# Two written-out decoder layers with a first norm that is loaded, summed and applied tile by tile

## What is computed

```python
c_act = jax.nn.silu(c)
for l in range(DEPTH):                                   # DEPTH = 2
    mod = (c_act @ ada_w[l] + ada_b[l]).reshape(bsz, 3, 3, D_MODEL)
    h = _rmsnorm(x, ffn1_norm[l]) * (1 + mod[:, 0, 1]) + mod[:, 0, 0]
    x = x + 0.5 * (1 + mod[:, 0, 2]) * ((silu(h @ w1[l]) * (h @ w3[l])) @ w2[l])
    h = mod2(RMSNorm(x));  x = x + (1 + g2) * mixer(h)   # RG-LRU and two attentions
    h = mod3(RMSNorm(x));  x = x + 0.5 * (1 + g3) * swiglu(h)
return _rmsnorm(x, final_norm) * (1 + fm[:, 1]) + fm[:, 0]
```

## Time and profile before

| | us |
|---|---|
| median of 3 runs (lowest to highest) | 2819.32 (2815.86 to 2821.81) |
| the profiled execution, by its own time | 2812.3 |
| its span in the profile | 2810.6 |
| PE, DVE, ACT, POOL busy | 2696.0, 1258.1, 1059.6, 1171.8 |

### The profile page before, as it was taken

The page is one execution under the profiler, slowest core; times in us unless marked ns, Lnnn a source line. Parts: engine busy times, 40 slices in busy tenths (PEclk is TensorE's granted clock), DMA queues, the critical chain, the costliest instruction groups (busy, mean ns, idle before and its releaser), DMA issues.

```text
span 2810.6 us, 35297 instructions
## 1 busy us (share of the span) xinstructions
PE 2696.0 (96%) x13124; PEld 2253.0 (80%) x13124; DVE 1258.1 (45%) x1608; ACT 1059.6 (38%) x1593; POOL 1171.8 (42%) x471
## 2 busy tenths in 40 slices
PE   3999999999999999999989999999999999999998
PEld 3888888878878878888888888888888788888886
DVE  6565337865442234411145553477545421453111
ACT  5222236644443244222242222466443432523223
POOL 2555544532223444454435554354222244355443
PEclk9999999999999999999999999999999999999999
DMA  6555532221112323533335555222122123253333
GB/s 219 210 187 203 173 116 95 88 71 60 61 54 75 98 91 127 173 92 103 97 131 191 198 189 167 89 88 91 60 60 61 46 90 98 77 187 127 103 93 97
DMA packets 91302, 325.73 MB, mean 116 GB/s; under 512 B 10096, under 2 KB 12528, under 8 KB 90864
## 3 DMA queue, kind: packets, MB, share of 16 engines
q1 hardware_dynamic: 91120, 323.35, 35.4%
HBM read 321.21 MB, written 2.10 MB: 115 GB/s over the span
## 4 chain that ended last, share of the span: by engine, by line
issue 54%; POOL 33%; PE 12%; POOLq 0%; ACT 0%; DVE 0%; ACTq 0%; DVEq 0%
POOL w_lo L406 32%; PE bank L1189 4%; PE bank L1187 4%; PE bank L1188 4%; POOL wab_lo L412 1%; POOLq L404 0%; ACT fin L765 0%; POOL tmp L389 0%; DVE fin L1180 0%; DVE x L828 0%; ACTq L113 0%; PE bank L1244 0%; ACT rstd L450 0%; ACT tmp L442 0%; ACT rstd L447 0%
## 5 line engine op out<-in xcount | busy, mean ns | idle before, releaser
L406 POOL TENSOR_TENSOR w_lo<-raw,w_hi 128x1024 fp32r<-128x1024 f32 x443 | 1152.4, 2611 | 1541.5 <-ACT w_hi L436 1540.9
L1187 PE MATMUL bank<-h_hi,w_hi 128*128 128x512 f32 x2240 | 876.3, 391 | 0.5
L1188 PE MATMUL bank<-h_lo,w_hi 128*128 128x512 f32 x2240 | 873.4, 390 | 0.0
L1189 PE MATMUL bank<-h_hi,w_lo 128*128 128x512 f32 x2240 | 873.1, 390 | 0.0
L436 ACT ACTIVATE w_hi<-raw 128x1024 fp32r<-128x1024 f32 x443 | 467.2, 1057 | 987.7 <-PE bank L1189 904.8
L1187 PEld LDWEIGHTS bank<-h_hi,w_hi 128*128 128x128 f32 x2240 | 421.6, 188 | 89.1 <-POOL w_lo L406 1.3
L1189 PEld LDWEIGHTS bank<-h_hi,w_lo 128*128 128x128 f32 x2240 | 421.1, 188 | 88.7
L1188 PEld LDWEIGHTS bank<-h_lo,w_hi 128*128 128x128 f32 x2240 | 421.5, 188 | 87.2
L776 DVE CUSTOM_DVE_ANT_0 ada<-ada,c_act 128x1024 f32<-128x1024 f32 x144 | 254.0, 1771 | 266.5 <-DMA ada<-ada_w 266.5
L1189 PE MATMUL bank<-g_hi,w_lo 128*128 128x512 f32 (+1 forms) x792 | 295.2, 373 | 0.0
L1188 PE MATMUL bank<-g_lo,w_hi 128*128 128x512 f32 (+1 forms) x792 | 292.4, 369 | 0.0
(11 more groups left out here) (208 smaller groups left out, 3057.3 us busy)
## 6 DMA issues: line engine op xcount, KB each, us to landing
raw<-w_units SPq DMA_DIRECT2D x443, 512.0 KB, 3.6
ada<-ada_w SPq DMA_DIRECT2D x144, 512.0 KB, 4.5
ada<-ada_w SPq DMA_DIRECT2D x8, 1024.0 KB, 16.5
x<-x_in SPq DMA_DIRECT2D x4, 512.0 KB, 7.3
wab_raw<-wab SPq DMA_DIRECT2D x2, 1024.0 KB, 5.7
y<-fin SPq DMA_DIRECT2D x8, 256.0 KB, 2.2
c_act<-c_rows SPq DMA_DIRECT2D x1, 512.0 KB, 3.7
vec<-vecs SPq DMA_DIRECT2D x3, 92.5 KB, 3.3
```

The costliest lines, as they stand in the source:

```text
L406: nc.gpsimd.tensor_tensor(w_lo[s][:, :, :], raw[u % RAW][:, :, :], w_hi[s][:, :, :].bitcast(F32), ALU.subtract).then_inc(unit_lo.sem, 1)
L1187: nc.tensor.matmul(o, wh, xh, start=start, stop=False, skip_group_check=True)
L1188: nc.tensor.matmul(o, wh, xl, start=False, stop=False, skip_group_check=True)
L1189: return nc.tensor.matmul(o, wl, xh, start=False, stop=stop, skip_group_check=True)
```

## The change

1. **The layers are written out.** `Fori` becomes a Python loop, so the code of both layers stands one behind the other and waits use constants. The loads, roundings and subtractions of units past the last (three of each at the end) are gone.
2. **Loads.** The rows of `ada_w` are reordered on the host so that piece `k` holds shift and scale of tile `k`. Piece 0 is issued ahead of `x`; each of the four loads of `x` has a semaphore of its own; units 0 to 3 follow, two of them into new buffers `raw0`, each with a piece behind it; pieces 5 to 7 come last.
3. **`c_act` in PSUM.** ACT copies it into banks 4 and 5, joined as `bank45`; the 16 first reductions read it there.
4. **Sum of squares and norm.** ACT squares each tile as it lands; DVE adds without reductions between; one matmul, one Ln and one Exp of 512 tokens replace the first half's.
5. **Tile by tile.** For each `k` DVE makes two reductions, adds the bias to two columns and forms one scale, then subtracts for `h_lo` of the tile before. The product with `rstd` is now POOL's, between the `w_lo` of units 0 to 3. ACT writes the unrounded `h` to PSUM banks 6 and 7. All of it handles 512 tokens at once.
6. **PE.** Each tile is multiplied with units 0 and 1 as it comes, and with units 2 and 3 three tiles later.

```diff
+        raw0 = [at(f"raw0_{i}", 65536 + 4096 * i, [P, UB, P]) for i in range(2)]
...
-        bank = [ctx.enter_context(nc.psum_tensor(f"bank{i}", [P, T], F32)) for i in range(8)]
+        bank = [ctx.enter_context(nc.psum_tensor(f"bank{i}", [P, T], F32))[:, :] for i in range(4)]
+        bank45 = ctx.enter_context(nc.psum_tensor("bank45", [P, 2 * T], F32))
+        bank += [bank45[:, 0:T], bank45[:, T:2 * T]]
+        bank += [ctx.enter_context(nc.psum_tensor(f"bank{i}", [P, T], F32))[:, :] for i in (6, 7)]
...
-            for n in range(0, KD, 2):
-                sp.dma_start(x[:, n:n + 2, :], x_in[n:n + 2].rearrange("n p t -> p n t")).then_inc(x_loaded.sem, 16)
-            for g in range(16 // G0):
+            def first_ada(g):
                 sp.dma_start(ada0[g][:, :, :], ada_w[G0 * g:G0 * g + G0].rearrange("n p t -> p n t"))\
                     .then_inc(ada0_loaded[g].sem, 16)
-                if 2 <= g < 2 + RAW:
-                    sp.dma_start(raw[g - 2][:, :, :], w_units[g - 2]).then_inc(raw_loaded[g - 2].sem, 16)
-            with sp.Fori(0, DEPTH) as l:
-                for u in range(RAW, UNITS + RAW):
+
+            first_ada(0)
+            for n in range(0, KD, 2):
+                sp.dma_start(x[:, n:n + 2, :], x_in[n:n + 2].rearrange("n p t -> p n t"))\
+                    .then_inc(x_loaded[n // 2].sem, 16)
+            for u in range(RAW):
+                sp.dma_start(raw[u][:, :, :], w_units[u]).then_inc(raw_loaded[u].sem, 16)
+                first_ada(u + 1)
+            for u in range(RAW, RING):
+                sp.dma_start(raw0[u - RAW][:, :, :], w_units[u]).then_inc(raw0_loaded[u - RAW].sem, 16)
+                first_ada(u + 1)
+            for g in range(RING + 1, KD):
+                first_ada(g)
+            for l in range(DEPTH):
+                for u in range(RING if l == 0 else RAW, UNITS + RAW):
...
-            for u in range(RAW, AHEAD):
-                load_unit(DEPTH, u, u)
...
-            with gp.Fori(0, DEPTH) as l:
-                for u in range(UNITS):
+            def first_lo(u):
+                gp.wait_ge(unit_hi.sem, u + 1)
+                src = raw[u] if u < RAW else raw0[u - RAW]
+                nc.gpsimd.tensor_tensor(w_lo[u][:, :, :], src[:, :, :], w_hi[u][:, :, :].bitcast(F32),
+                                        ALU.subtract).then_inc(unit_lo.sem, 1)
+
+            def first_xr(k):
+                if k >= 2:
+                    gp.wait_ge(hf_0.sem, k - 1)
+                nc.gpsimd.tensor_tensor(tmp[k % 2][:, :], x[:, k, :], rstd[:, :], ALU.mult).then_inc(xr_0.sem, 1)
+
+            first_lo(0)
+            gp.wait_ge(rstd_0.sem, 1)
+            first_xr(0)
+            first_lo(1)
+            first_xr(1)
+            first_xr(2)
+            first_lo(2)
+            first_xr(3)
+            first_lo(3)
+            for k in range(4, KD):
+                first_xr(k)
+            for l in range(DEPTH):
+                for u in range(RING if l == 0 else 0, UNITS):
                     lo(l, u)
                     for c in range(KD):
                         if u == U_X(c) + 3:
                             wab_lo_part(l, c)
-            for u in range(AHEAD):
-                lo(DEPTH, u)
...
+            def first_h(k):
+                act.wait_ge(nscale_0.sem, k + 1)
+                act.wait_ge(xr_0.sem, k + 1)
+                shift, scale = mod[:, k:k + 1], nscale[:, 0, k:k + 1]
+                A(h_hi[:, k, :], tmp[k % 2][:, :], ACT.Identity, bias=shift, scale=scale).then_inc(hh_0.sem, 1)
+                if k >= 2:
+                    act.wait_ge(hl_0.sem, k - 1)
+                A(bank[6 + k % 2][:, :], tmp[k % 2][:, :], ACT.Identity, bias=shift, scale=scale).then_inc(hf_0.sem, 1)
...
+            act.wait_ge(silu_c.sem, 1)
+            A(bank45[:, :], c_act[:, :], ACT.Copy).then_inc(c_wide.sem, 1)
...
-            act.wait_ge(x_loaded.sem, 16 * KD // 2)
-            for n in range(KD - 1):
-                square(0, -1, n)
-            square(0, -1, KD - 1, HALF[0])
-            square(0, -1, KD - 1, HALF[1])
-            norm(0, -1, 0)
-            for u in range(-AHEAD, 0):
-                tick(0, u)
-            with act.Fori(0, DEPTH) as l:
-                h_round(l, -1, 0, 0, ((2, 0),))
-                norm(l, -1, 1)
-                h_round(l, -1, 0, 1)
+            for n in range(KD):
+                if n % 2 == 0:
+                    act.wait_ge(x_loaded[n // 2].sem, 16)
+                if n >= 3:
+                    act.wait_ge(sqsum_0.sem, n - 2)
+                A((tmp[n % 2] if n else sqsum)[:, :], x[:, n, :], ACT.Square).then_inc(sq_0.sem, 1)
+            first_tick(0)
+            act.wait_ge(sumsq_0.sem, 1)
+            A(rstd[:, :], bank[BS][:, :], ACT.Ln, bias=eps_col[:, 0:1], scale=1.0 / D).then_inc(ln_0.sem, 1)
+            act.wait_ge(ln_0.sem, 1)
+            A(rstd[:, :], rstd[:, :], ACT.Exp, scale=-0.5).then_inc(rstd_0.sem, 1)
+            first_tick(1)
+            for k in range(KD):
+                first_h(k)
+                if k in (1, 2):
+                    first_tick(k + 1)
+            for l in range(DEPTH):
+                if l:
+                    h_round(l, -1, 0, 0, ((2, 0),))
+                    norm(l, -1, 1)
+                    h_round(l, -1, 0, 1)
...
             dve.wait_ge(silu_c.sem, 1)
+            dve.wait_ge(c_wide.sem, 1)
             dve.wait_ge(vec_loaded.sem, 16)
-            def ada_tile_0(a):
-                g, i = divmod(a, G0)
-                dve.wait_ge(ada0_loaded[g].sem, 16)
-                V.tensor_tensor_reduce(ada0[g][:, i, :], ada0[g][:, i, :], c_act[:, :], 1.0, 0.0, ALU.mult, ALU.add,
-                                       mod[:, a:a + 1]).then_inc(ada_done.sem, 1)
-            for n in range(KD - 1):
-                square_add(0, -1, n)
-                ada_tile_0(n)
-            for h in range(2):
-                square_add(0, -1, KD - 1, HALF[h], h)
-            ada_tile_0(KD - 1)
-            for a in range(KD, 16):
-                ada_tile_0(a)
-            mod_bias(0, 0, 0, 16)
-            scale_col(0, 0, V_NORM1, 0)
-            with dve.Fori(0, DEPTH) as l:
-                h_tiles(l, -1, 0)
-                h_tiles(l, -1, 1)
+
+            def first_ada(k):
+                dve.wait_ge(ada0_loaded[k].sem, 16)
+                for i in range(G0):
+                    V.tensor_tensor_reduce(ada0[k][:, i, :], ada0[k][:, i, :], bank45[:, :], 1.0, 0.0, ALU.mult,
+                                           ALU.add, mod[:, KD * i + k:KD * i + k + 1]).then_inc(ada_done.sem, 1)
+                dve.wait_ge(ada_done.sem, G0 * k + 2)
+                V.tensor_tensor(mod[:, k:k + KD + 1:KD], mod[:, k:k + KD + 1:KD],
+                                vec[:, V_ADAB + k:V_ADAB + k + KD + 1:KD], ALU.add).then_inc(mod_0.sem, 1)
+                dve.wait_ge(mod_0.sem, k + 1)
+                V.scalar_tensor_tensor(out=nscale[:, 0, k:k + 1], in0=mod[:, KD + k:KD + k + 1], scalar=1.0,
+                                       in1=vec[:, V_NORM1 + k:V_NORM1 + k + 1], op0=ALU.add,
+                                       op1=ALU.mult).then_inc(nscale_0.sem, 1)
+
+            def first_rest(k):
+                dve.wait_ge(hf_0.sem, k + 1)
+                V.tensor_tensor(h_lo[:, k, :], bank[6 + k % 2][:, :], h_hi[:, k, :].bitcast(F32),
+                                ALU.subtract).then_inc(hl_0.sem, 1)
+
+            first_ada(0)
+            for n in range(1, KD):
+                dve.wait_ge(sq_0.sem, n + 1)
+                if n > 1:
+                    dve.wait_ge(sqsum_0.sem, n - 1)
+                V.tensor_tensor(sqsum[:, :], sqsum[:, :], tmp[n % 2][:, :], ALU.add).then_inc(sqsum_0.sem, 1)
+            for k in range(1, KD):
+                first_ada(k)
+                first_rest(k - 1)
+            first_rest(KD - 1)
+            for l in range(DEPTH):
+                if l:
+                    h_tiles(l, -1, 0)
+                    h_tiles(l, -1, 1)
...
+            def first_h(k, js):
+                if js[0] == 0:
+                    pe.wait_ge(hh_0.sem, k + 1)
+                for j in js:
+                    for w in (w_hi, w_lo):
+                        if k == 0:
+                            pe.wait_ge((unit_hi if w is w_hi else unit_lo).sem, j + 1)
+                        nc.tensor.matmul(bank[j][:, :], w[j][:, k, :], h_hi[:, k, :], start=k == 0 and w is w_hi,
+                                         stop=False, skip_group_check=True)
+                if js[0] == 0:
+                    pe.wait_ge(hl_0.sem, k + 1)
+                for j in js:
+                    i = nc.tensor.matmul(bank[j][:, :], w_hi[j][:, k, :], h_lo[:, k, :], start=False, stop=k == KD - 1,
+                                         skip_group_check=True)
+                    if k == KD - 1:
+                        i.then_inc(unit_done.sem, 1)
+
             def ffn(l, s):
                 u0 = U_FFN[s]
-                after_norm(l, u0, 2 * s - 1)
```

(16 more changed lines are left out.)

## The result

| | kernel before | changed kernel |
|---|---|---|
| median of the comparison (4 executions each) | 2817.67 us | 2792.52 us |
| ratio, 95% interval | | 0.991, 0.9895 to 0.9925 |
| profiled execution (span) | 2812.3 us (2810.6) | 2793.99 us (2792.2) |
| median of all executions of this study | 2815.6 us (75) | 2792.0 us (15) |

The change is faster, by 25.2 us between the first medians, 18.3 us between the two profiled executions and 23.6 us between the medians of all executions. The change is under 1%, but the interval of the ratio is clear of 1. The three measured savings and the forecast's 20.1 don't agree with each other, and most of this part is about why.

What follows compares the result with a forecast made beforehand. The prediction took PE's matmuls to bound the kernel. Savings of 15.9 us at the start and 4.2 at the layer boundary, 20.1 in sum, off the 2819.3 us median gave 2799 us, range 2793 to 2810.

Steps and rivals of the forecast that it cites:

- What bounds the kernel, and the two places: Whole kernel: bound by PE's matmuls, busy 2696.0 of 2810.6 us; idle time to win at the start and the layer boundary.
- The front of the start: Loads, squares, adds and norm at the start: last add ends at 16.7, Ln at 19.1, `rstd` ready at 20.5 against 29.2.
- POOL's product and the reductions: First norm: POOL's 512-column product takes 1.28 us; DVE's reductions, reading `c_act` from PSUM, take 1.14 us, not held by POOL.
- held too: Rival, first norm: POOL also holds DVE's reductions, the pair starts at 69, time 2810 us; chance 0.12.
- The small operations: First norm, DVE: POOL holds these at tiles 1 and 3, scales at 24.6 instead of 21.5 and 34.8 instead of 31.4.
- the hold at tile 1: First norm, DVE: small operations wait for POOL's product, then unit 1's `w_lo`; scale at 24.6 instead of 21.5.
- PE and the pair: End of the start: unit 0 ends at 52.0, the next pair of units starts at 58.3 instead of 74.16, 15.9 us saved.
- the prediction's 6.0 us: From unit 0's end over `tick`, Silu, two roundings and two `w_lo` to the next pair's first matmul: 6.0 us.
- The rival of half clock: Rival, start: PE's clock stays at half, the pair starts at 61.5 to 63.5, time 2802 to 2804 us; chance 0.15.
- The boundary: Between the layers: without the loop's branch PE's pause shrinks from 7.1 to 2.7 us; 4.2 us saved, ends 3.2 and 4.6.
- The rest: Elsewhere: removed register instructions save 0, up to 1.5 us; the dead subtractions at the end save 0.
- the saving is taken off the median: Final step: 20.1 us is subtracted from the 2819.3 us median of three runs, not the profiled 2812.3, giving 2799 us.

Runs made afterwards that it cites:

- The caught execution: The kernel before with nothing changed, one profiled execution from the slow tail of its executions: 2821.91 us.

## Why the prediction was right, and where it failed

*What bounds the kernel, and the two places.* Right: outside of the start and the boundary the two traces hold the same matmuls, and their waits of over 1 us are the same to 0.1 us.

*The front of the start.* Nearly: the adds alternate with ACT's squares and end at 17.6 instead of 16.7, so Ln is at 19.8 instead of 19.1 and `rstd` at 21.1 instead of 20.5.

*POOL's product and the reductions.* 1.28 us was interpolated, and 1.28 is the mean of the eight. The reduction's 1.14 from start to start is right too, and so is its reason: the rival "held too" was built as a kernel and costs 9.5 us, where the prediction had put 11 (2810 against 2799).

*The small operations.* Right in kind and in number (two tiles), wrong in place and size: not tiles 1 and 3 with 3.1 and 3.4 us, but 3 and 4 with 1.3 and 1.5. At both, the first operation waits for the end of what POOL is at, and the second for a whole product of 1.27. Tile 1 got through at 20.94, just before POOL's first product at 21.22. That the times came out near all the same is partly luck: the prediction left out that the subtraction for tile 0 stands in DVE's queue ahead of tile 2's reductions. DVE waited there for 2.80 us, for POOL's first product and ACT's two passes, nearly the 3.1 us that the hold at tile 1 was to cost. Free tiles follow each other in 3.27 us instead of 3.4. `h_lo` of tile 7 was ready at 49.1 instead of 50.4.

*PE and the pair.* Unit 0's last matmul ended at 50.9 instead of 52.0, and the prediction's 6.0 us from there give 56.9. The collision of the two `w_lo` with DVE's reductions, for which 0.3 was added, took 0.9 (5.63 against 4.77 for the two). The pair started at 57.83, 58.22 and 57.97 in three profiles, 74.24 on average in seven of before: 16.2 us saved, forecast 15.9.

*The clock at the start.* The rival of half clock came true in part: 0.62 from 38 to 42 us, after a wait of 3.1 us. No cost of it is seen. The chain over ACT and POOL, not PE, set the pair (1.35 us of waiting ahead of it), and PE had caught up before: its first matmul of tile 7 came 1.75 us behind that tile's `h_hi` (49.52 against 47.77), just as in the kernel with its reductions in SBUF, where no such stretch lay in the start (58.09 against 56.34).

*The boundary.* Forecast 4.2, measured 4.3 in the traces. *The rest* was put at 0 and up to 1.5, and seven profiles of before and three of the changed kernel show nothing systematic in the two stretches between.

*The number.* 16.2 + 4.3 = 20.5 us against a sum of 20.1. **The step that failed is the last: "the saving is taken off the median".** The profiled execution less the sum is 2792.2 us, within 0.3 of the result; the median of three less the sum is 2799. The prediction noted that the profile lay 7.0 us below the median and outside of the three, and didn't draw the conclusion that the three were too few to say where the kernel stands (75 executions: 2811 to 2826, median 2815.6). With that median it would have been 2795.5. That the profiled execution less the sum hits the result is luck in part, since that execution was one of the fast ones. Of the 6.7 us between forecast and result, 3.7 are this base, 0.4 the sum, and 3.1 what is left below; 0.5 goes the other way, since the first four executions of the changed kernel lay that much above the median of all 15.

*What is left* is 23.6 - 20.5 = 3.1 us between the medians of all executions. The interval (21.0 to 24.8) nearly reaches the sum. With the layers alone written out the medians lie 6.4 us apart where the traces give 4.3, so 2.1 of the 3.1 come with the loop's end and 1.0 with the start (17.2 against 16.2). The caught execution shows one way in which executions of before are late by 5.9 us where the changed kernel was never seen late, but the 14 late ones of 75 raise the median by 1.0 us only (2814.6 without them). Where the rest comes from stays open.

## What to carry to other kernels

Before a saving of under 1% is taken off anything, find out how far executions of the unchanged kernel lie apart; if the profiled execution and the median differ by as much as a term of the sum, the base is the least certain number in it. Where DVE and GpSimd work side by side in SBUF, try one input of DVE's long operations in PSUM, and don't forget the one-column operations between them: here they paid for what was left of the operation that they met, up to its whole length. PE's pauses of 4.29 us cost themselves and then the clock behind them; extra matmuls in such a pause won the second part back, while in shorter ones, with an operand due right behind, no gain was seen.

## What the runs showed of the hardware

PE's clock. In 20 profiles each stretch at half clock (1.2 GHz) behind the start began inside a pause of PE of more than 1.4 us or within 4 us of its end, and none without one; behind 45 pauses of 1.0 to 1.4 us there was none. Which pauses are followed by one differs from execution to execution: leaving out the last pause ahead of the end, of 88 pauses of 1.5 us 37 were, of 40 of 1.8 us none, of 158 of 2.2 us 105, of 34 of 4.29 us all, at 3.4 to 10.2 us each. What decides isn't shown; it isn't the length alone, since those of 1.8 us had none. At the same pause of 4.29 us the same kernel had 3.4 us once and 10.2 another time. As PE does half its work in such a stretch, that moves an execution by up to 3.4 us at one place, and the work at half clock, 39 to 52 us in the profiles of before, is most of what sets its executions between 2812 and 2817 us apart.

The order of two engines at a shared lock. 0.1 to 0.2 us between the starts of DVE's subtraction and POOL's `w_lo` decided about 4.4 us of PE's time, in the one execution caught.

An instruction on one or two columns beside POOL took 1.18 us (a product), 2.10 (a `w_lo`), and 0.16 alone: its own size didn't matter, what it met did.
